# Hybrid attention block on one core: the K and Q weight splits of the first phase's second pass are given in three portions

## The reference

```python
h = rms_norm(x, norm_mix_pre[l])
proj = h @ w_in[l]
qa, ka, va, qd, kd, vd = jnp.split(proj, IN_SPLITS, axis=-1)
qa = apply_rope(qa.reshape(b, s, SWA_Q_HEADS, HEAD_DIM), cos, sin)
ka = apply_rope(ka.reshape(b, s, SWA_KV_HEADS, HEAD_DIM), cos, sin)
out_a = swa_sink_attention(qa, ka, va, swa_sinks[l])   # window of two chunks of 64, a sink per head
qd = apply_rope(qd.reshape(b, s, 2 * DIFF_HEADS, HEAD_DIM), cos, sin)
kd = apply_rope(kd.reshape(b, s, 2 * DIFF_HEADS, HEAD_DIM), cos, sin)
out_b = diff_attention(qd, kd, vd, lam, diff_subln[l], lambda_init)
mixed = jnp.concatenate([out_a, out_b], axis=-1) @ w_out[l]
x = x + rms_norm(mixed, norm_mix_post[l])
h = rms_norm(x, norm_ffn_pre[l])
f = (jax.nn.silu(h @ w_gate[l]) * (h @ w_up[l])) @ w_down[l]
x = x + rms_norm(f, norm_ffn_post[l])
```

## Time and profile before

| what | us |
|---|---|
| median of 3 runs | 2595.13 |
| lowest, highest | 2592.71, 2597.39 |
| the profiled execution | 2592.32 |
| its span on the core | 2590.5 |
| PE busy | 2384.5 (92%) |
| DVE busy | 1630.0 (63%) |
| ACT busy | 1203.6 (46%) |
| POOL busy | 678.1 (26%) |

### The profile page before, as it was taken

The page is one execution under the profiler, slowest core; times in us unless marked ns, Lnnn a source line. Parts: engine busy times, 40 slices in busy tenths (PEclk is TensorE's granted clock), DMA queues, the critical chain, the costliest instruction groups (busy, mean ns, idle before and its releaser), DMA issues. The chain is left out here.

```text
span 2590.5 us, 36663 instructions
## 1 busy us (share of the span) xinstructions
PE 2384.5 (92%) x11796; PEld 1979.3 (76%) x11796; DVE 1630.0 (63%) x3093; ACT 1203.6 (46%) x2731; POOL 678.1 (26%) x810
## 2 busy tenths in 40 slices
PE   7999997996898888699769999999999999999998
PEld 5888886885777677577558888888888888888886
DVE  5676776554888888433365555556776655554877
ACT  5555564332666666433343333334554333334444
POOL 1223222221566566354401111110000111111001
PEclk9999998997999999899989999999999999999999
DMA  5111122444232221446463323247675333326774
GB/s 175 48 52 50 47 87 67 132 133 155 69 104 71 76 86 37 161 163 222 163 227 113 103 94 114 82 138 245 195 264 195 107 101 106 113 75 221 245 269 146
DMA packets 222105, 340.08 MB, mean 131 GB/s; under 512 B 20320, under 2 KB 119648, under 8 KB 220128
## 3 DMA queue, kind: packets, MB, share of 16 engines
q1 hardware_dynamic: 221920, 337.86, 39.2%
HBM read 234.50 MB, written 103.28 MB: 130 GB/s over the span
## 5 line engine op out<-in xcount | busy, mean ns | idle before, releaser
L2410 PE MATMUL ff_psum<-ff_hop,ff_a_hi 128*128 128x512 f32 x1760 | 542.4, 389 | 4.3 <-issue 4.3
L2410 PEld LDWEIGHTS ff_psum<-ff_hop,ff_a_hi 128*128 128x128 f32 x1760 | 330.0, 188 | 74.4 <-issue 5.9
L2410 PE MATMUL ff_psum<-ff_hop,ff_a_lo 128*128 128x512 f32 x880 | 342.4, 389 | 0.0
L2434 PE MATMUL ff_psum<-ff_a_hi 128*128 128x512 f32 x616 | 239.6, 389 | 0.0
L2434 PE MATMUL ff_psum<-ff_a_lo,ff_a_hi 128*128 128x512 f32 x616 | 239.6, 389 | 0.0
L2434 PE MATMUL ff_psum<-ff_a_hi,ff_a_lo 128*128 128x512 f32 x616 | 239.6, 389 | 0.0
L2073 ACT ACTIVATE ff_a_hi<-ff_w_raw 128x512 fp32r<-128x512 f32 x220 | 138.0, 629 | 212.8 <-PE ff_psum L2410 190.7
L2410 PE MATMUL ff_psum<-hop,ff_a_hi 128*128 128x512 f32 x704 | 219.0, 392 | 17.0 <-DVE ff_a_lo L2186 17.0
L1222 ACT ACTIVATE da_probs<-da_psum,da_bias 128x512 f32<-128x512 f32 (+3 forms) x320 | 195.9, 621 | 74.0 <-DVE da_bias L1274 60.8
L2186 DVE TENSOR_TENSOR ff_a_lo<-ff_w_raw,ff_a_hi 128x512 fp32r<-128x512 f32 x220 | 161.6, 737 | 104.5 <-ACT ff_a_hi L2073 104.5
L2030 POOL TENSOR_TENSOR ff_go<-ff_go 128x512 f32<-128x512 f32 x22 | 28.4, 1290 | 682.8 <-DVE ff_go L2267 682.8
(11 more groups left out here) (235 smaller groups left out, 5350.9 us busy)
## 6 DMA issues: line engine op xcount, KB each, us to landing
g_s<-ff_go SPq DMA_DIRECT2D x154, 256.0 KB, 2.0
ff_ring<-g_s SPq DMA_DIRECT2D x154, 256.0 KB, 2.7
ff_ring<-in_w_down_dram SPq DMA_DIRECT2D x132, 256.0 KB, 3.1
ff_w_raw<-in_w_gate_dram SPq DMA_DIRECT2D x44, 512.0 KB, 3.6
ff_w_raw<-in_w_up_dram SPq DMA_DIRECT2D x44, 512.0 KB, 3.8
pp_x<-in_x_dram SPq DMA_DIRECT2D x32, 512.0 KB, 4.5
hop_s<-op_ht SPq DMA_DIRECT2D x8, 1792.0 KB, 7.5
ff_hop<-hop_s SPq DMA_DIRECT2D x10, 1024.0 KB, 9.2
```

What stands on the lines that cost most here:

```text
L2410: last = pe.matmul(ps[:, bank, :], w[:, unit % R, at], hop[i][:, h, c, :], start=(i in (0, 1, 6) and c == 0 and x_ == 0), stop=(c == 3 and ...
L2434: last = pe.matmul(ps[:, bank, :], g[:, unit % R, at], w[:, (unit + 1) % R, :], start=(i in (0, 1, 6) and c == 0 and x_ == 0), stop=(c == ...
```

## The change

The low and high halves of the K weights (step 15) and of the Q weights (step 16) are no longer made in one block of eight (on DVE in step 15, two of four) but in portions of three, three and two. `next_weights(i, first, end)` does nothing in other steps. On ACT the portions stand behind the first half of `exps(i - 1)`, behind the first `hi_a(i - 2)` and behind the second half of `exps`. On DVE they stand behind `maxima(i - 1)`, behind `lo_q` (in step 16, where there is none, behind `lo_a`), and behind `recips(i - 1)`. The lists of PE, POOL and SP are the same.

```diff
@@ -552,24 +552,28 @@
                 turned_hi(0)
                 square(1)
                 weights_hi(2, 2 * KC)
+                def next_weights(i, first, end):
+
+                    if i in (TILES - 1, TILES):
+                        at = (3 if i < TILES else 4) * KC
+                        weights_hi(at + first, at + end)
+
                 for i in range(PASS + 1):
                     u = i - TILES
                     if i + 1 < PASS and i != 1:
                         turned_hi(i + 1)
                     if i + 2 < PASS:
                         square(i + 2)
-                    if i == TILES - 1:
-                        weights_hi(3 * KC, 4 * KC)
-                    if i == TILES:
-                        weights_hi(4 * KC, 5 * KC)
                     if attending(i - 3):
                         copy_o(i - 3)
                     if attending(i - 1):
                         exps(i - 1, (0, 1))
+                    next_weights(i, 0, 3)
                     if i < TILES:
                         copy_v(i)
                     if attending(i - 2):
                         hi_a(i - 2, (0, 1))
+                    next_weights(i, 3, 6)
                     if i < TILES:
                         hi_q(i)
                     elif u >= 1:
@@ -578,6 +582,7 @@
                         copy_dv(0)
                     if attending(i - 1):
                         exps(i - 1, (2, 3))
+                    next_weights(i, 6, KC)
                     if i == 1:
                         turned_hi(2)
                     if 0 < i < TILES:
@@ -732,12 +737,16 @@
                 turned_lo(0)
                 scale_x(1)
                 weights_lo(2, 2 * KC)
+                def next_weights(i, first, end):
+
+                    if i in (TILES - 1, TILES):
+                        at = (3 if i < TILES else 4) * KC
+                        weights_lo(at + first, at + end)
+
                 for i in range(PASS + 1):
                     u = i - TILES
                     if i + 1 < PASS and i != 1:
                         turned_lo(i + 1)
-                    if i == TILES:
-                        weights_lo(4 * KC, 5 * KC)
                     if i < TILES:
                         rope_q(i)
                     elif i < PASS:
@@ -747,8 +756,7 @@
                         rope_k(i)
                     if attending(i - 1):
                         maxima(i - 1)
-                    if i == TILES - 1:
-                        weights_lo(3 * KC, 7 * KC // 2)
+                    next_weights(i, 0, 3)
                     if attending(i - 3):
                         add_o(i - 3)
                     if i < TILES and i != 1:
@@ -761,10 +769,10 @@
                         lo_q(i)
                     elif u >= 1:
                         lo_d("q", u - 1)
-                    if i == TILES - 1:
-                        weights_lo(7 * KC // 2, 4 * KC)
+                    next_weights(i, 3, 6)
                     if attending(i - 1):
                         recips(i - 1)
+                    next_weights(i, 6, KC)
                     if i == 1:
                         turned_lo(2)
                     if 0 <= u < TILES:
```

## The result

| | median us | lowest, highest | runs |
|---|---|---|---|
| before | 2595.68 | 2592.71, 2600.2 | 18 |
| after | 2601.88 | 2597.4, 2607.32 | 18 |

The changed kernel is **slower** by a little: ratio 1.0022, 95% interval 1.0015 to 1.0030, which is 5.7 us (3.9 to 7.8). The forecast was 2594.6 with a range to 2599.5; the time lies above the range and the change went the other way. Its profiled execution has a span of 2599.8 us for 2590.5.

What follows compares the result with a forecast made beforehand. PE bounds the kernel, without slack behind step 17, so only that step's start counts: 6.1 us won at `attend(13)` shrink to 0.8, then 0.5 earlier at `dq(0)`. From median 2595.13: 2594.6 us, range 2591.0 to 2599.5, 70%.

Steps and rivals of the forecast that it cites:

- The order and step 15's first portion: Step 15: DVE waits for splits behind `exps(14)`; `add_o(12)` 2.1 us later, PE's wait 4.2 becomes 6.3, `turn_x(17)` at 381.7.
- Five K splits to 386.1: Step 15, DVE: five splits left from 382.3 at 0.66 us each, `recips` between; last K piece 4.8 us later.
- x and `square(18)`: Step 16: x of tile 18 follows the last K split; `square(18)` 7.5 us behind it, at 393.6, load taken as 6.3.
- `dk(0)` does not wait for the weights: PE's `dk(0)` starts at 382.5, reaches its last slice five microseconds on, so does not wait for the K splits.
- What is left of the gain at `add_o(13)`: Step 16: 6.1 us won at `attend(13)` shrink to 0.8, with three Q splits ahead of `add_o(13)`: 400.6 for 401.42.
- The last portion: Step 16: DVE's last Q low half ready at 409.9, `dq(0)` ends at 410.7 for 411.18, last slices at full clock.
- the criterion named in the prediction: If step 17 starts before 408 or behind 417, the working is wrong: check x's landing, then the clock of `dk(0)`.
- The sum without the collision: The prediction's whole sum over steps 15 and 16: `dq(0)` ends 0.5 us earlier, giving 2594.6.
- half clock through three projections: Slower rival: after the 6.3 us wait the clock stays low through `v(15)`, `dk(0)`, `dq(0)`; 10.5 later, 2605.6; 4%.
- x over 5 us late: Far end of the late-x rival (13% for x's landing time), each microsecond beyond 6.3 costing one; counted under slower.
- the 7% for slower by over 0.2%: Chance given to a slower result, made of half clock through three projections and x over 5 us late.
- the bounds: Below: x in 4.5 us, end 1.9 earlier; above: all of `dq(0)` at half clock, 2.8 later; 2593.2 to 2597.9.

Runs made afterwards that it cites:

- e4: Kernel before with one SP DMA moved: x of tile 18 loaded in step 15 ahead of the Q pieces' loads; 2590.22 us, ratio 0.9977.
- e1: Changed kernel with one swap on DVE: the last portion (two splits) stands ahead of `recips`, not behind it; 2594.12 us, ratio 0.9994.
- e3: Changed kernel with POOL's scaling of the probabilities of tiles 14 and 15 cut to one column of each head; 2595.66 us, ratio 1.0002.
- e7: e4 with DVE's eight Q splits moved from ahead of `rope_d` to behind `add_o(13)`; 2585.34 us, ratio 0.9966.
- e8: e7 with DVE's first four K splits moved from ahead of `add_o(12)` to behind `rope_k(15)`; 2582.5 us, ratio 0.9956.
- e6: Changed kernel with the edits of e1 and e4 in one (last portion ahead of `recips`, x of tile 18 early); 2592.61 us, ratio 0.9991.

## Why the prediction was wrong, point by point

- *The order and step 15's first portion.* Right. DVE was idle 2.61 us (2.7 forecast), `add_o(12)` came at 370.26 + 1.19 = 371.45 (371.5), PE's wait was 6.26 (6.3). Left out was the clock: behind this wait the first four products of `v(15)` took 0.6 us more than before, so `turn_x(17)` came at 381.09 + 1.19 = 382.3 for 381.7. The chain of step 16 runs over DVE and the x tile, so this cost nothing there.
- *Five K splits to 386.1.* **This is the step that failed.** It gave each split 0.66 us wherever it stood. The last K split was ready at 387.90 + 1.19 = 389.1, 3.0 later, since it was held by POOL's scaling. The prediction said "SP's and POOL's lists stay as they are", and never asked what POOL does at the new places of DVE's splits.
- *x and `square(18)`.* The mechanism was right, and e4 shows it. The size was off both ways: 3.0 later by the split; 1.2 sooner, since `square(18)` followed the last split by 6.3 for 7.5, of which 1.0 is the time from x's issue (5.3 for 6.3); so 395.4 for 393.6.
- *`dk(0)` does not wait for the weights.* Wrong by 0.94 us, from the same cause.
- *What is left of the gain at `add_o(13)`.* 0.8 us forecast (400.6), but it came at 402.51 for the 401.42 of before, a loss of 1.1.
- *The last portion.* Forecast ready at 409.9. DVE's pair ended at 413.77 + 1.19 = 415.0, PE waited 3.87 in `dq(0)`, the last two slices ran at half clock where the prediction took the full level, and step 17 began at 418.6 for 412.0. Of these 6.6 us 1.9 were there at `turn_a(14)`, 3.3 are the held Q split and 1.4 the clock behind the wait. Same failed step, second place; the criterion named in the prediction, step 17 behind 417, spoke, but it pointed to x and to the clock first, which was the wrong place to look.
- *The sum without the collision.* Forecast 0.5 us earlier. With the pairs out of POOL's way (e1) the two steps are 1.2 shorter, with the scaling cut (e3) 0.9; the measured ratios of both hold no change. So the rest of the working stands.
- *The rivals.* The rival on the slower side was half clock through three projections; `v(15)` was back at the full level in its second slice (products 0.23 apart from 375.46 on), and that rival did not happen. The other one on that side, x over 5 us late, did not either: x took less time than assumed. So the 7% for slower by over 0.2% came true by neither of its causes; the held split was not among the rivals, and the bounds had no row for it.

The row was there to be read. In the trace of the kernel before, the rows of the splits' source line by region (durations min/median/max in ns):

```profile
L614 DVE SCALAR_TENSOR_TENSOR pp_wa_lo<-pp_w_raw,pp_g_col,pp_wa_hi x16: 744/747/752, 8.0 to 380.5; 128x512 fp32r<-128x512 f32 x16
L614 DVE SCALAR_TENSOR_TENSOR pp_wv_lo<-pp_w_raw,pp_g_col,pp_wv_hi x16: 740/744/1751, 32.0 to 395.2; 128x512 fp32r<-128x512 f32 x16
```

And from its timelines of DVE and POOL, step 1, the block with the odd one and POOL's rotation beside it:

```profile
36.00 3.74 DVE L614 SCALAR_TENSOR_TENSOR pp_wv_lo<-pp_w_raw,pp_g_col,pp_wv_hi 128x512 fp32r<-128x512 f32 x4
...
36.16 1.70 POOL L388 TENSOR_TENSOR pp_rot<-pp_part_c,pp_part_s 128x512 f32<-128x512 f32 x1 [9.52 <-DVE pp_part_s L627]
```

One of 32 splits took 1.75 for 0.74, beside a POOL instruction that took 1.70 for 1.29. Its neighbours in the block and in the group hide it in a mean. A rotation of 1.3 us costs one split 1.0; a scaling of 3.6 costs one 3.3.

The Trainium skill, SBUF — State Buffer, section "SBUF: two separate sides", says that DVE and GpSimd share a port pair under an exclusive lock, which a DVE operation with two SBUF inputs takes against a GpSimd operation that reads SBUF; whoever starts first has it for the whole instruction. The traces agree in both directions (4.02 and 4.09 for 0.75 on DVE, 4.00 for 3.60 on POOL), and DVE's operations with one input in PSUM run beside the scaling at full speed, as in the kernel before:

```profile
381.62 1.29 DVE L707 TENSOR_TENSOR pp_at_lo<-pp_psum,pp_at_hi 128x512 fp32r<-128x512 f32 x2
...
381.66 3.61 POOL L409 TENSOR_TENSOR pp_probs<-pp_probs,pp_recip 128x2048 f32<-128x2048 f32 x1 [8.44 <-DVE pp_recip L686]
```

The two `turned_lo` at 383.56 lie wholly within POOL's 3.61 us and take 1.29, as they do at 415.44, where POOL does nothing. No run here varied the split's own inputs, so that it is the second SBUF input that matters is not shown by a run of its own; it rests on these rows and the page. By that rule a split of each pair behind `recips` is held for what is left of POOL's 3.6 us, which DVE's list, shown ahead of the prediction, already told.

## What to carry to other kernels

When an instruction of DVE with both inputs in SBUF is moved, look at what POOL does at its new place, and above all at what the instruction ahead of it releases: here `recips` released POOL's 3.6 us, and a split of the pair behind it paid 3.3. Read the maximum beside the median of a group; one odd instruction in 32 showed beforehand that a split can be held. And where a block of work stands ahead of a critical wait, moving it behind the consumer that needs nothing of it gave more than cutting it into portions inside the chain (e7 and e8 against e6, all with x early).

## What was not expected of the hardware

The exclusion works in both directions, also for small instructions: in e8 POOL's `rotate_k` and its two reciprocal-root steps, beside four splits, took 0.90, 0.52 and 0.94 us for 0.46, 0.19 and 0.55. There the wait is hidden, for `scale_x` stands behind the splits anyway.

```profile
368.31 0.90 POOL L396 TENSOR_TENSOR pp_rot_k<-pp_rot_kc,pp_rot_ks 128x128 f32<-128x128 f32 x1 [4.87 <-DVE pp_rot_ks L629]
369.30 0.52 POOL L164 TENSOR_SCALAR pp_rstd<-pp_ss 128x1 f32<-128x1 f32 x1
369.90 0.94 POOL L166 TENSOR_TENSOR pp_rstd<-pp_rstd,pp_half 128x1 f32<-128x1 f32 x1
```
